# MLP columns with the high and low activations streamed as one 512-column operand

## What is computed

```python
# first block, after its mixers
a = rmsnorm(h, norm2[i])
h = h + (jax.nn.silu(a @ w_gate[i]) * (a @ w_up[i])) @ w_down[i]
...
# second block, two layers: mixer, then
def sq_relu_mlp(h, w_up, w_down):
    return jnp.square(jax.nn.relu(h @ w_up)) @ w_down
...
x = x + sq_relu_mlp(rmsnorm_2(x, mlp_norm[layer]), w_up[layer], w_down[layer])
```

## Time and profile before

| | |
|---|---|
| time, median of 3 runs | 865.14 us (864.61 to 865.71) |
| the profiled execution | 865.72 us, of which its span is 864.0 us |
| TensorE matmuls busy | 851.8 us |
| VectorE, ScalarE busy | 606.7 us, 469.6 us |
| granted TensorE clock, mean of the span | 0.999 |
| HBM read and written over the span | 173 GB/s |

### The profile page before, as it was taken

The page is one execution under the profiler, slowest core; times in us unless marked ns, Lnnn a source line. Parts: engine busy times, 40 slices in busy tenths (PEclk is TensorE's granted clock), DMA queues, the critical chain, the costliest instruction groups (busy, mean ns, idle before and its releaser), DMA issues.

```text
span 864.0 us, 19329 instructions
## 1 busy us (share of the span) xinstructions
PE 851.8 (99%) x7298; PEld 818.8 (95%) x7298; DVE 606.7 (70%) x997; ACT 469.6 (54%) x754; POOL 94.6 (11%) x147
## 2 busy tenths in 40 slices
PE   9999999999999999999999999999999999999997
PEld 8988899999999999788999999999999999999996
DVE  5776567666666687878876666668979966666665
ACT  6646766444434485448754444446786744444443
POOL 4320002000000039511100000002110100000001
PEclk9999999999999999999999999999999999999999
DMA  7532346665565648524465555554544465555551
GB/s 260 169 123 98 98 147 227 192 211 183 185 208 183 194 164 235 170 91 135 179 208 194 194 194 194 194 192 151 171 147 151 168 220 192 192 190 187 194 184 49
DMA packets 44290, 151.61 MB, mean 175 GB/s; under 512 B 5588, under 2 KB 6868, under 8 KB 44244
## 3 DMA queue, kind: packets, MB, share of 16 engines
q1 hardware_dynamic: 41040, 145.00, 50.8%
q0 software_dynamic: 2400, 4.89, 1.8%
q10 hardware_dynamic: 804, 1.06, 0.4%
HBM read 148.14 MB, written 1.05 MB: 173 GB/s over the span
## 4 chain that ended last, share of the span: by engine, by line
PE 86%; DVE 6%; ACT 3%; POOL 2%; issue 1%; DMA 1%; SPq 0%; DVEq 0%; ACTq 0%; POOLq 0%
PE bank L1411 26%; PE bank L1412 25%; PE bank L1413 25%; DVE alo L985 2%; PE bank L1805 1%; DVE wlo L961 1%; PE bank L1441 1%; PE bank L1433 1%; PE bank L1577 1%; PE bank L1554 1%; POOL shared L493 1%; PE bank L1895 1%; DMA shared<-zpad 1%; PE bank L1525 1%; DVE h L995 1%
## 5 line engine op out<-in xcount | busy, mean ns | idle before, releaser
L1411 PE MATMUL bank<-ahi,whi 128*128 128x256 f32 (+1 forms) x1392 | 395.0, 284 | 0.7 <-DVE alo L979 0.5
L1413 PE MATMUL bank<-ahi,wlo 128*128 128x256 f32 (+1 forms) x1392 | 387.0, 278 | 0.0
L1412 PE MATMUL bank<-alo,whi 128*128 128x256 f32 (+1 forms) x1392 | 386.8, 278 | 0.0
L961 DVE TENSOR_TENSOR wlo<-raw,whi 128x1024 fp32r<-128x1024 f32 x272 | 331.1, 1225 | 25.5 <-ACT whi L541 25.4
L541 ACT ACTIVATE whi<-raw 128x1024 fp32r<-128x1024 f32 x272 | 281.5, 1052 | 86.9 <-PE bank L1413 74.8
L1411 PEld LDWEIGHTS bank<-ahi,whi 128*128 128x128 f32 x1392 | 261.9, 188 | 5.5 <-DVE alo L979 2.4
L1412 PEld LDWEIGHTS bank<-alo,whi 128*128 128x128 f32 x1392 | 261.6, 188 | 0.4
L1413 PEld LDWEIGHTS bank<-ahi,wlo 128*128 128x128 f32 x1392 | 261.6, 188 | 0.0
L1411 PE MATMUL bank<-hidhi,whi 128*128 128x256 f32 x704 | 194.5, 276 | 0.6 <-DVE wlo L961 0.6
L1413 PE MATMUL bank<-hidhi,wlo 128*128 128x256 f32 x704 | 194.4, 276 | 0.0
L1412 PE MATMUL bank<-hidlo,whi 128*128 128x256 f32 x704 | 194.4, 276 | 0.0
(11 more groups left out here) (236 smaller groups left out, 725.9 us busy)
## 6 DMA issues: line engine op xcount, KB each, us to landing
raw<-in_slabs SPq DMA_DIRECT2D x272, 512.0 KB, 3.6
shared<-in_convw POOLq DMA_DIRECT2D x4, 512.0 KB, 6.8
shared<-zpad POOLq DMA_DIRECT2D x48, 35.5 KB, 3.5
raw<-in_slabs SPq DMA_DIRECT2D x8, 128.0 KB, 5.1
vtok<-in_gatew POOLq DMA_DIRECT2D x2, 512.0 KB, 4.9
out<-y SPq DMA_DIRECT2D x4, 256.0 KB, 2.3
h<-in_xT ACTq DMA_DIRECT2D x3, 272.0 KB, 5.2
h<-in_xT SPq DMA_DIRECT2D x1, 272.0 KB, 3.8
```

What stands on the lines that cost most here:

```text
L961: dve.tensor_tensor(wlo[:, n % R, :, :], raw[:, n % R, :, :], whi[:, n % R, :, :].bitcast(F32), ALU.subtract).then_inc(lo_done, 1)
L1411: pe.matmul(dst, hi, xh, start=start, stop=False, skip_group_check=True)
L1412: pe.matmul(dst, hi, xl, start=False, stop=False, skip_group_check=True)
L1413: return pe.matmul(dst, lo, xh, start=False, stop=stop, skip_group_check=True)
```

## The change

In all columns of the MLPs but the first ones, `column` gives way to `wide_column`. `ahi` and `alo` become two halves of one tile, `both`, at the same addresses. For chunk k one matmul streams both halves (2 x 256 columns) against the high weights into the whole bank: columns 0 to 255 gather high by high, columns 256 to 511 high by low. A second matmul adds low weights by high activations to the left half. So a column is 8 matmuls of 512 columns and 8 of 256.

The two halves are added afterwards: ScalarE copies the right half to `part` (in the tile `prob`; `low_part`), VectorE adds the left half to it (`whole`) and waits for its own result before it goes on with the factor. `low_part` stands behind ScalarE's split for that slab, and in the last gated block the second one stands behind one more split. Rows, first columns and the columns outside of the MLPs are as they were. There are 21 x 2 widened columns in the gated MLP and 30 in each of the others.

```diff
+W_MLP2 = 2 * (FF1 - 1)
+W_MLP3 = W_MLP2 + FF2 - 2
...
-        ahi = sb("ahi", [P, KC * STRIDE_A], F32R)
-        alo = sb("alo", [P, KC * STRIDE_A], F32R)
+        both = sb("both", [P, 2, KC * STRIDE_A], F32R)
+        ahi, alo = both[:, 0, :], both[:, 1, :]
...
+        part = prob[:, 2:4, 0:SEQ]
...
+        def both_chunk(k):
+            c = STRIDE_A * k + SHIFTED.get(k, 0)
+            return both[:, :, c + NMETA:c + T1]
...
+            def low_part(i, bank, n, q):
+
+                act.wait_ge(slab_used, n + 1 + q)
+                act.activation(part[:, i, :], bank[:, SEQ:2 * SEQ], ACT.Copy).then_inc(part_ready, 1)
+
             def swiglu(f, n, q=0, row=True):
 
                 split_ahead(n, 3 * q)
+                if f >= 1:
+                    low_part(0, aux_bank if f == 1 else gemm_bank[0], n, 12 * q)
                 act.wait_ge(gemm_evac, E_MLP1 + 2 * f + 1 + 8 * q)
                 act.activation(hid[:, f % 2, :], hidg[:, f % 2, :], ACT.Silu).then_inc(act_hid, 1)
                 if f == FF1 - 1:
                     split_ahead(n + 1, 3 * q)
+                if f >= 1:
+                    low_part(1, gemm_bank[1], n + 1, 12 * q)
                 act.wait_ge(prod_ready, f + 1 + 4 * q)
...
             def squared_relu(f, n, e0, q=0, row=True):
 
                 split_ahead(n, q)
+                if f >= 2:
+                    low_part(f % 2, col_bank(f), n, 4 * q)
                 act.wait_ge(gemm_evac, e0 + f + 1 + 2 * q)
...
+            def whole(dst, bank, i, w):
+
+                dve.wait_ge(part_ready, w + 1)
+                dve.tensor_tensor(dst, bank[:, 0:SEQ], part[:, i, :], ALU.add).then_inc(part_added, 1)
+                dve.wait_ge(part_added, w + 1)
+
             def swiglu(f, n, q=0, row=True):
 
                 dve.wait_ge(slab_used, n + 1 + 12 * q)
                 src = aux_bank if f == 1 else gemm_bank[0]
-                dve.tensor_tensor(hidg[:, f % 2, :], src[:, NMETA:T1], rstd[:, NMETA:], ALU.mult).then_inc(gemm_evac, 1)
+                g, u = hidg[:, f % 2, :], hidu[:, f % 2, :]
+                if f >= 1:
+                    whole(g, src, 0, 2 * f - 2 + 8 * q)
+                dve.tensor_tensor(g, g if f >= 1 else src[:, NMETA:T1], rstd[:, NMETA:], ALU.mult).then_inc(gemm_evac, 1)
                 split_ahead(n, 3 * q)
                 dve.wait_ge(slab_used, n + 2 + 12 * q)
-                dve.tensor_tensor(hidu[:, f % 2, :], gemm_bank[1][:, NMETA:T1], rstd[:, NMETA:], ALU.mult).then_inc(gemm_evac, 1)
+                if f >= 1:
+                    whole(u, gemm_bank[1], 1, 2 * f - 1 + 8 * q)
+                dve.tensor_tensor(u, u if f >= 1 else gemm_bank[1][:, NMETA:T1], rstd[:, NMETA:], ALU.mult)\
+                   .then_inc(gemm_evac, 1)
...
-            def squared_relu(f, n, e0, m0, q=0, row=True):
+            def squared_relu(f, n, e0, m0, w0, q=0, row=True):
 
                 dve.wait_ge(slab_used, n + 1 + 4 * q)
-                dve.scalar_tensor_tensor(hid[:, f % 2, :], col_bank(f)[:, NMETA:T1], 0.0, rstd[:, NMETA:],
+                u = hid[:, f % 2, :]
+                if f >= 2:
+                    whole(u, col_bank(f), f % 2, w0 + f - 2 + 2 * q)
+                dve.scalar_tensor_tensor(u, u if f >= 2 else col_bank(f)[:, NMETA:T1], 0.0, rstd[:, NMETA:],
                                          ALU.max, ALU.mult).then_inc(gemm_evac, 1)
...
+            def wide_column(n, bank, q=0):
+
+                slab_ready(n, q)
+                for k in range(KC):
+                    pe.matmul(bank[:, :].rearrange("p (a b) -> p a b", a=2), whi[:, n % R, k, :], both_chunk(k),
+                              start=(k == 0), stop=False, skip_group_check=True)
+                    ins = pe.matmul(bank[:, 0:SEQ], wlo[:, n % R, k, :], chunk(ahi, k, NMETA), start=False,
+                                    stop=(k == KC - 1), skip_group_check=True)
+                ins.then_inc(slab_used, 1)
+
...
-                column(n, aux_bank if f == 1 else gemm_bank[0], 3 * q)
+                wide_column(n, aux_bank if f == 1 else gemm_bank[0], 3 * q)
                 pe.wait_ge(gemm_evac, E_MLP1 + 2 * f + 8 * q)
-                column(n + 1, gemm_bank[1], 3 * q)
+                wide_column(n + 1, gemm_bank[1], 3 * q)
...
-                column(base + 2, col_bank(2))
+                wide_column(base + 2, col_bank(2))
...
                     pe.wait_ge(gemm_evac, q * 2 + (e0 + f - 1))
-                    column(n, gemm_bank[f % 2], q)
+                    wide_column(n, gemm_bank[f % 2], q)
...
                     pe.wait_ge(gemm_evac, e0 + f - 1)
-                    column(base + FF2 - 3 + f, gemm_bank[f % 2])
+                    wide_column(base + FF2 - 3 + f, gemm_bank[f % 2])
```

More of the change, by code:

```diff
@@ L310, in build @@
         act_hid, hid_hi, hid_lo = sem("act_hid"), sem("hid_hi"), sem("hid_lo")
+        part_ready, part_added = sem("part_ready"), sem("part_added")
         fl_zero, fl_w, fl_parts, fl_copied = sem("fl_zero"), sem("fl_w"), sem("fl_parts"), sem("fl_copied")
@@ L1304, in squared_relu, with squared_relu_mlp @@
                     split_ahead(n + 1, q)
-            def squared_relu_mlp(base, e0, m0):
+            def squared_relu_mlp(base, e0, m0, w0):
                 for f in range(3):
-                    squared_relu(f, base + f, e0, m0)
+                    squared_relu(f, base + f, e0, m0, w0)
                 split_ahead(base + 4)
@@ L1311, in squared_relu_mlp @@
                     for j in range(2):
[L1312 to L1315, removed]
+                        squared_relu(3 + j, base + 5 + 2 * j, e0, m0, w0, it)
+                squared_relu(FF2 - 3, base + 2 * FF2 - 7, e0, m0, w0)
+                squared_relu(FF2 - 2, base + 2 * FF2 - 5, e0, m0, w0, row=False)
+                squared_relu(FF2 - 1, base + 2 * FF2 - 4, e0, m0, w0)
                 split_ahead(base + 2 * FF2 - 2)
-            squared_relu_mlp(MLP2, E_MLP2, FF1)
+            squared_relu_mlp(MLP2, E_MLP2, FF1, W_MLP2)
             link(dve.memset(proj[:, 8:16, NMETA - LRU_T + 1:NMETA], 0.0))
@@ L1390, in _ @@
             dve.wait_ge(rstd_ready, RS0[N_MLPC] + 1)
-            squared_relu_mlp(MLP3, E_MLP3, FF1 + FF2)
+            squared_relu_mlp(MLP3, E_MLP3, FF1 + FF2, W_MLP3)
             acc_add(ACC_MLP3, NSLABS - 1, N_FINAL, None)
```

## The result

The changed kernel takes **885.96 us** (885.40 to 887.58), beside 865.58 us (864.61 to 865.97) for the kernel before, run beside it: a ratio of 1.0239, 95% interval 1.0228 to 1.0250. It is 20.4 us slower, and 12 us above the forecast.

The account below looks back on a forecast made before the run. The prediction took the distance between TensorE's matmul starts as the bound: +5.3 us for the widened columns' chunks and +3.6 us at the MLPs' ends, +8.9 us on the median of 865.14, gave 874.0 us, range 860 to 880.

Parts of the forecast that it names:

- the mid-stream: Middle of the MLPs: added copies and additions make TensorE wait 0 us, up to 1 us, since 2.9 us is spare.
- D: Rival: the copies stop TensorE in the middle of the MLPs, forecast plus 3 to 10 us; chance 0.06.
- 512 columns: Widened MLP columns: one 512-column matmul costs 0.234 us; with its narrow neighbour, +0.0065 us a chunk, +5.3 us over 816.
- A: Rival: the surplus belongs to each start, so 512 columns take 0.220 us, a chunk 0.3335; total 861.4 us; chance 0.20.
- B: Rival: a wide matmul takes exactly two of the good pace, 0.2267 us, a chunk 0.340; total 866.7 us; chance 0.12.
- The narrow one between two wide: Widened MLP columns: the 256-column matmul between two 512-column ones takes 0.115 us, making a chunk 0.349 us against 0.3425.
- The ends: Last rows of the three MLPs: TensorE waits 2.0, 0.8 and 0.8 us for the low part; sum 3.6 us.
- The rows at 2.72 us: Rows of the MLPs, which the change leaves alone: they were to stay at 2.72 us each, adding nothing.
- rival C: Wide columns leave TensorE in the slow pace: chunk 0.3515 us, some 80 MLP rows at 2.82; total 884 us; chance 0.12.

## Why the prediction was wrong

**What bounds the kernel, and the mid-stream: right.** There is no wait in mid-stream, VectorE is busy for 128.1 of 180 us, and D did not happen.

**512 columns: right in the number, for a reason not seen.** 0.234 us forecast from the earlier trace rows, 0.2341 measured. A (0.220) is never seen, and the kernel with 384 and 128 columns shows why: at the slow pace the surplus goes with the columns. B's 0.227, twice the fast pace, is what a single wide one takes out of the fast pace (0.226); it fails as a forecast because TensorE does not stay there. So 0.234 is the price of the slow pace and not of the wide form as such. The Trainium skill, page "TensorE: Matmul & The Clock Gate", section "Back-to-back issue gap", would give 216 ns here by its formula for a single matmul's gap; the shortest distance behind a 512-column fp32r matmul in these runs is 225 ns, and the measurement decides.

**The narrow one between two wide: too low.** Taken at 0.115, its mean in a steady column is 0.1184, just above the upper bound of 0.1175. With the wide ones at 0.2334 there, a chunk is 0.3518 against 0.349 us: 816 x 0.0028 = 2.3 us.

**The ends: right in kind, a little high.** The waits are 1.7, 0.6 and 0.6 us for 2.0, 0.8 and 0.8. In the first MLP the order of ScalarE and VectorE is the forecast one, only tighter. From the timelines of after:

```profile
311.06 0.36 ACT L758 ACTIVATE prob<-bank 128x256 f32<-128x256 f32 x1
```

```profile
313.92 0.42 DVE L1216 TENSOR_TENSOR hidlo<-y,hidhi 128x256 fp32r<-128x256 f32 x1
```

```profile
314.39 0.39 PE L1448 MATMUL bank<-hidhi,whi 128*128 128x256 f32 x1 [1.66 <-DVE hidlo L1216]
```

The copy stands behind the split, the low part ends 2.9 us later, and TensorE has then stood idle for 1.66 us, against 0.18 us of cover in the earlier trace rows.

**The rows at 2.72 us: the step that failed.** The sum had no term for them ("a row 2.72" in the forecast), and 8.7 us fell there. I had the mechanism with its place and price: rival C gave 884 us, and its two signs (chunk 0.3515, rows at 2.82) are what the trace shows, 0.3518 and 2.826. I gave it 0.12, because in the earlier trace rows a column that begins unevenly settles after six matmuls. That was read as "TensorE settles by itself". The kernel without the shift shows that it does not: there no column settles. The first six matmuls of the earlier trace rows are what the shift of chunk 0 costs, and they come with the return to the fast pace; a wide column doesn't pass that on to the row. And the earlier trace rows, a whole row at 0.1175 with nothing to wait for, answer the question whether a pace is kept. Rival C says so, but the sum took from them the price of the wide form alone. Read so, C was the likeliest case, at 884 us.

From 874.0 to 886.0: rows 8.7, chunks 2.3, ends -0.8, the kernel before 0.4 higher beside it; 1.4 us remain, of which 0.5 are between the profiled execution and the median.

**What stays open.** Why a 64-byte shift restores the fast pace, why it does so at one pass and not at another, and why a wide matmul tips it, was not found: the profile shows starts and no reason between them. A stop of TensorE can change the pace too, as before the last rows of after; in the kernel with the additions alone the first MLP's first row, at 142.9 us, stands behind a shorter stop and is slow. That the reason lies in how TensorE reads its operands fits the effect of their places, and is argued, not shown.

## What to carry to other kernels

When a stream of matmuls is all that counts, compare its start-to-start distance with the same shape elsewhere in the trace; if two values occur, ask first what sets the one that the kernel enjoys, and whether the change takes that away from code that it doesn't touch. A surplus per matmul is not a surplus per instruction until two sizes have been compared: here it went with the columns, and fewer, longer matmuls had nothing to win. And a single measured distance, such as that of the earlier trace rows, can belong to the pace it was taken in and not to the shape. A step lengthened by 0.9 us is free where 2.9 us of cover stand and is paid in full where the cover is one row, so price the ends apart from the middle.

## What was unexpected of the hardware

- Narrow fp32r matmuls (256 columns) have at least three steady distances at a granted clock of 1.00: 0.1133, 0.1177 and 0.120 us, with the same instructions. A shift of 64 bytes of one chunk in eight decides between the first two over whole MLPs (865.5 or 883.2 us), one of the hidden tiles brings the third.
- The pace is a state: it holds over columns and rows, and one 512-column matmul as a column's last chunk turns it over, from fast to slow and from slow to fast (rows of 2.826 and 2.723 us in turn). That matmul takes 0.226 us out of the fast pace and 0.233 out of the slow one.
- The shift of chunk 0 doesn't end a slow pace at every pass: of two shifted columns that begin slow in one trace, one takes 2.83 us and stays slow, the other 2.76 and leaves fast.
- Six narrow matmuls on chunks 0 and 1 at a column's end run slowly themselves and leave the row behind them fast.
- A 128-column matmul starts its successor after 0.059 us, and that one then takes 0.169 us for 256 columns in place of 0.118.
